# Heads enter attention in fours instead of pairs

## The reference, cut to what matters

```python
# block 1, 16 heads of 64 (256 keys are one block, so this is plain causal softmax): "moba"
p = softmax(where(k_pos <= q_pos, (q @ k.T) * 64 ** -0.5, -inf));  o = p @ v;  mix = o @ w_o

# block 2, heads 0 to 7, stick-breaking: "sb"
z = (q @ k.T) * 64 ** -0.5
log_keep = where(mask, log_sigmoid(-z), 0)                   # mask: key strictly before query
later = cumsum(log_keep, reverse=True) - log_keep            # sum over the later keys
w = where(mask, exp(log_sigmoid(z) + later), 0);  o = w @ v

# block 2, heads 8 to 15, forgetting attention: "fox" (q and k are normed per head)
z = (q @ k.T) * 64 ** -0.5 + F[query] - F[key]               # F: cumulative log of the forget gate
p = softmax(where(mask, z, -inf));  o = p @ v
mix = concat(all heads) @ w_o
```

## Time and profile before

| | |
|---|---|
| median of 3 runs | 814.82 us (813.75 to 815.11) |
| the profiled execution | 814.42 us, of which the span of the trace is 812.2 |
| busy in the span | TensorE 798.2, VectorE 647.5, ScalarE 483.8, GpSimd 21.1 us |
| granted TensorE clock | 0.997 of full speed on average |
| memory traffic | 179.44 MB, 221 GB/s on average |

### The profile page before, as it was taken

How to read it: one execution, slowest core, us unless ns; L and a number is a source line. 1 busy time by engine, 2 the same in 40 slices (tenths; PEclk the granted TensorE clock), 3 DMA queues, 4 the chain that set the end, 5 groups by cost and what they waited for, 6 DMA issues and landing times.

```text
span 812.2 us, 16860 instructions
## 1 busy us (share of the span) xinstructions
PE 798.2 (98%) x6810; PEld 777.2 (96%) x6810; DVE 647.5 (80%) x1385; ACT 483.8 (60%) x1008; POOL 21.1 (3%) x53
## 2 busy tenths in 40 slices
PE   8999999999999999999999999899999999999998
PEld 7999998999999999999999999889889999999998
DVE  5889887988899886999988887977667896775551
ACT  6755566776666566745554646665655775555440
POOL 1000000000000000000000000700000000000000
PEclk9999999999999999999999999999999999999999
DMA  9777683666656987499998887545334578655540
GB/s 292 261 240 241 219 286 113 206 203 208 206 191 199 324 299 261 157 322 325 360 327 297 298 259 223 163 135 175 124 109 152 167 261 271 209 184 196 194 157 27
DMA packets 150014, 179.44 MB, mean 221 GB/s; under 512 B 5681, under 2 KB 139569, under 8 KB 149937
## 3 DMA queue, kind: packets, MB, share of 16 engines
q1 hardware_dynamic: 147680, 177.22, 65.5%
q10 hardware_dynamic: 1232, 1.11, 0.4%
q0 software_dynamic: 1024, 0.03, 0.1%
HBM read 177.27 MB, written 1.05 MB: 220 GB/s over the span
## 4 chain that ended last, share of the span: by engine, by line
PE 77%; DVE 4%; ACT 3%; issue 1%; DVEq 0%; ACTq 0%
PE bank L1396 24%; PE bank L1399 23%; PE bank L1400 23%; DVE wlo L979 1%; PE bank L1385 1%; PE bank L1503 1%; PE bank L1387 1%; PE bank L1386 1%; PE bank L1487 1%; PE bank L1520 0%; PE bank L1417 0%; PE bank L1449 0%; ACT whi L736 0%; PE bank L1466 0%; DVE yb L1019 0%
## 5 line engine op out<-in xcount | busy, mean ns | idle before, releaser
L979 DVE TENSOR_TENSOR wlo<-raw,whi 128x512 fp32r<-128x512 f32 x528 | 342.9, 684 | 66.9 <-ACT whi L736 66.4
L736 ACT ACTIVATE whi<-raw 128x512 fp32r<-128x512 f32 x528 | 306.9, 622 | 96.6 <-PE bank L1400 85.4
L1396 PE MATMUL bank<-A,whi 128*128 128x256 f32 x1152 | 323.6, 281 | 2.8 <-DVE wlo L979 2.0
L1399 PE MATMUL bank<-A,whi 128*128 128x256 f32 x1152 | 319.5, 277 | 0.1
L1400 PE MATMUL bank<-A,wlo 128*128 128x256 f32 x1152 | 319.1, 277 | 0.0
L1396 PEld LDWEIGHTS bank<-A,whi 128*128 128x128 f32 x1152 | 217.3, 189 | 4.4 <-DVE wlo L979 2.2
L1399 PEld LDWEIGHTS bank<-A,whi 128*128 128x128 f32 x1152 | 217.2, 189 | 0.8 <-issue 0.5
L1400 PEld LDWEIGHTS bank<-A,wlo 128*128 128x128 f32 x1152 | 217.0, 188 | 0.0
L1396 PE MATMUL bank<-Hhi,whi 128*128 128x256 f32 x528 | 146.0, 276 | 0.0
L1400 PE MATMUL bank<-Hhi,wlo 128*128 128x256 f32 x528 | 145.7, 276 | 0.0
L1399 PE MATMUL bank<-Hlo,whi 128*128 128x256 f32 x528 | 145.7, 276 | 0.0
(11 more groups left out here) (160 smaller groups left out, 956.7 us busy)
## 6 DMA issues: line engine op xcount, KB each, us to landing
mring<-in_w_mod SPq DMA_DIRECT2D x72, 512.0 KB, 6.4
raw<-in_ffn_w_up SPq DMA_DIRECT2D x22, 1024.0 KB, 5.1
raw<-in_w_gate SPq DMA_DIRECT2D x22, 1024.0 KB, 5.6
raw<-in_w_up SPq DMA_DIRECT2D x22, 1024.0 KB, 5.8
raw<-in_w_down SPq DMA_DIRECT2D x16, 1024.0 KB, 5.8
raw<-in_w_in SPq DMA_DIRECT2D x12, 1024.0 KB, 5.8
raw<-in_moba_w_qkv SPq DMA_DIRECT2D x11, 1024.0 KB, 6.4
raw<-in_ffn_w_down SPq DMA_DIRECT2D x8, 1024.0 KB, 7.1
```

What stands on the lines that cost most here:

```text
L736: act.activation(whi[:, i % SPL, k0:k1, 0:width], raw[:, i % RAW, k0:k1, 0:width], ACT.Copy).then_inc(s_whi, 1)
L979: dve.tensor_tensor(lo, raw[:, i % RAW, k0:k1, 0:width], hi.bitcast(F32), ALU.subtract).then_inc(s_wlo, 1)
L1396: pe.matmul(o, hi, xh, start=kg == 0 and not (j and halved(g)), stop=False)
L1399: pe.matmul(o, hi, xl, start=False, stop=False)
```

## The change

Four heads enter together. `scores` multiplies all four in one step, first the one pair of heads, then the other; `values` does so too, into the two halves of `O_BANK`, with one copy by ScalarE and one by VectorE behind it. Only the fours that begin with head 12 have two `values` steps of two heads. The steps in between remain steps of one head, at ages given by the table `AGES`: for moba and fox as before (the second pair three turns after the first), for sb one head every second turn, with `values` at age 12. The next four enters when the one before has age 6 or more. `scores` waits until the banks of all four heads are free, and in qkv3 until the last group that used two banks is evicted (`last_raw`). FA and FB are cleared to zero and get ones in 4 rows at 0 and at 64, and their product takes 64 rows. `UNLOCK` and the due turn of `vturn` are moved by one or two turns. The core of the diff:

```diff
--- before.py
+++ after.py
@@
-LAST_AGE = 6
+AGES = {"sb": ((0, 2, 4, 6), (2, 4, 6, 8), (4, 6, 8, 10), 12), "moba": ((0, 0, 3, 3), (2, 3, 5, 6), (3, 4, 6, 7), 9)}
+AGES["fox"] = AGES["moba"]
-UNLOCK = {("qkv3", 512): 5, ("qkv3", 2048): 3, ("qkv3", 2304): 3}
+UNLOCK = {("qkv3", 512): 7, ("qkv3", 2048): 5, ("qkv3", 2304): 3}
@@ Plan.lay
         def advance(n, age):
             kind, ph, h = self.heads[n]
+            passes, sums, turned, last = AGES[kind]
+            early = h == 12
             if age == 0:
                 st.put("scores", n)
-            if age in (3, 4):
-                m = n + age - 3
-                st.put("later" if kind == "sb" else "turn", m)
-                self.w_of[m] = len(self.w_of) + 1
-            if age in (2, 3):
-                st.put("stsum" if kind == "sb" else "scale", n + age - 2)
-            if age == LAST_AGE:
-                while h // 2 not in v_ready:
-                    pend(force=True)
-                st.put("values", n)
-                o_ready.add(h // 2)
+            for first, size, at in ((n, 2, turned[1] + 2), (n + 2, 2, last)) if early else ((n, 4, last),):
+                if age == at:
+                    while h // 2 not in v_ready:
+                        pend(force=True)
+                    st.put("values", first, size)
+                    for k in range(first, first + size):
+                        self.values_of[k] = (first, size)
+                        o_ready.add(self.heads[k][2] // 2)
+            for k in range(4):
+                if age == turned[k]:
+                    st.put("later" if kind == "sb" else "turn", n + k)
+                    self.w_of[n + k] = len(self.w_of) + 1
+                if age == sums[k]:
+                    st.put("stsum" if kind == "sb" else "scale", n + k)
+            for k in range(4):
+                if age == passes[k]:
+                    st.put("passes", n + k)
@@ enter, attend
-            self.heads += [waiting.pop(0), waiting.pop(0)]
+            self.heads += [waiting.pop(0) for _ in range(4)]
...
-            if waiting and (not flight or flight[-1][1] > 2):
+            if waiting and (not flight or flight[-1][1] >= 6):
                 enter()
             turns[0] += 1
-            pend(not any(pair[1] in (3, 4) for pair in flight))
+            pend(not any(four[1] in AGES[self.heads[four[0]][0]][2] for four in flight))
...
-                    pending.append(("vturn", ph, base, turns[0] + 2))
+                    pending.append(("vturn", ph, base, turns[0] + 3))
@@ gpsimd, spread_f
-                pool.memset(FA[:, :, :].bitcast(F32), 1.0).then_inc(s_fset, 1)
-                pool.memset(FB[:, :, :].bitcast(F32), 1.0).then_inc(s_fset, 1)
+                pool.memset(FA[:, :, :].bitcast(F32), 0.0).then_inc(s_fset, 1)
+                pool.memset(FB[:, :, :].bitcast(F32), 0.0).then_inc(s_fset, 1)
                 pool.wait_ge(s_fset, 2)
+                for r0 in (0, 64):
+                    pool.memset(FA[r0:r0 + 4, :, :].bitcast(F32), 1.0).then_inc(s_fset, 1)
+                    pool.memset(FB[r0:r0 + 4, :, :].bitcast(F32), 1.0).then_inc(s_fset, 1)
+                pool.wait_ge(s_fset, 6)
@@ scalar, values (the vector engine's in the same way)
-            def values(n):
-                f = heads[n][2] // 2
-                need.wait_ge(s_val, n // 2 + 1)
-                act.activation(Ohi[:, f, :], banks[O_BANK][:, 0:S], ACT.Copy).then_inc(s_ohi, 1)
+            def values(n, size):
+                need.wait_ge(s_val, val_of[n])
+                o, src = heads_out(n, size)
+                act.activation(Ohi[:, o, :], src, ACT.Copy).then_inc(s_ohi, 1)
@@ tensor, scores
-                for m in (n - 4, n - 3):
+                for m in range(n - 4, n):
                     if m in soft:
                         need.wait_ge(s_exp, soft[m])
                     elif m in stick:
                         need.wait_ge(s_lb, stick[m])
+                if ph == "qkv3":
+                    emptied(need, last_raw)
...
+                    for two in (four[0:2], four[2:4]):
+                        for o0, o1, k0, q0 in ((P, 3 * P, 0, 0), (0, P, P, P)):
+                            for b, q, k in two:
+                                pe.matmul(b[:, o0:o1], k[:, k0:k0 + P], q[:, q0:S], start=q0 == 0, stop=False)
+                    for b, q, k in four:
+                        pe.matmul(b[:, 0:S], identb[:, :], negs[:, :].unsqueeze(1).broadcast_to([P, 2, P]), start=False,
+                                  stop=True).then_inc(s_scores, 1)
                     return
...
                 if kind == "fox":
...
-                            r = slice(64 * e, 64 * e + 4)
-                            ins = pe.matmul(pair[e][0][:, o0:o1], FA[r, i, q0:q0 + P], FB[r, i, 0:o1 - o0], start=False, stop=o0 > 0)
+                                ins = pe.matmul(two[e][0][:, o0:o1], FA[rows[e], i, q0:q0 + P], FB[rows[e], i, 0:o1 - o0], start=False, stop=o0 > 0)
@@ tensor, values
                 for t, o0, w0, w1 in ((0, 0, P, 3 * P), (1, P, 0, P)):
-                    for e in range(2):
-                        o, w = banks[O_BANK][64 * e:64 * e + 64, o0:S], W8[:, 2 * ((n + e) % 4) + 1, w0:w1]
-                        ins = pe.matmul(o, Vn[:, t, (h + e) * 64:(h + e) * 64 + 64], w, start=t == 0, stop=t == 1)
+                    for e in range(size):
+                        c = e // 2 * S
+                        o, w = banks[O_BANK][64 * (e % 2):64 * (e % 2) + 64, c + o0:c + S], W8[:, 2 * ((n + e) % 4) + 1, w0:w1]
+                        ins = pe.matmul(o, Vn[:, t, (h + e) * 64:(h + e) * 64 + 64], w, start=t == 0 and e < 2, stop=t == 1 and e >= size - 2)
```

More of the change, by code:

```diff
@@ L525, in build_program @@
         t_use = {step: k for k, step in enumerate(s for s in st.list if s[0] in ("turn", "later", "vturn", "qkn"))}
+        val_of = {n: nth("values", *plan.values_of[n]) for n in range(len(heads))}
+        val_of_tile = {(heads[n][1], heads[n][2] // 2): val_of[n] for n in range(len(heads))}
         soft = {n: k + 1 for k, n in enumerate(m for m, h in enumerate(heads) if h[0] != "sb")}
@@ L961, in _ @@
             part_of = {"hi": weights, "ain": a_in, "gq": norm_columns, "sq": squares, "norm": norm, "latey": late_hi, "modul": shift_hi,
[L962 removed]
+                       "ccol": condition, "evict": evict, "fpart": forget, "passes": first_pass, "turn": turned, "later": later,
                        "values": values, "vturn": v_turned, "qkn": qk_norm}
@@ L1314, in later, with values @@
                 dve.tensor_tensor(lb, lb, banks[T_BANK][:, 0:3 * P], ALU.add).then_inc(s_lsum, 1)
[L1316 to L1319, removed]
+            def values(n, size):
+                need.wait_ge(s_ohi, val_of[n])
+                o, src = heads_out(n, size)
+                dve.tensor_tensor(Olo[:, o, :], src, Ohi[:, o, :].bitcast(F32), ALU.subtract).then_inc(s_olo, 1)
             def qk_norm(base):
@@ L1332, in _ @@
                        "hcol": gates, "gq": first_columns, "mod": mod_dot, "modout": mod_out, "xscale": scale_x, "evict": evict, "fpart": forget,
-                       "scores": peaks, "scale": scale, "stsum": stick_sum, "later": later, "values": values, "qkn": qk_norm}
+                       "passes": peak, "scale": scale, "stsum": stick_sum, "later": later, "values": values, "qkn": qk_norm}
             for step in st.list:
@@ L1437, in scores @@
                     need.wait_ge(s_fmove, 16 * 32)
-                pair = [(head_bank(n + e), QKV[64 * e:64 * e + 64, place(ph, f), :], QKV[64 * e:64 * e + 64, place(ph, 8 + f), :]) for e in range(2)]
+                rows = (slice(0, 64), slice(64, P))
+                four = [(head_bank(n + e), QKV[rows[e % 2], place(ph, f + e // 2), :], QKV[rows[e % 2], place(ph, 8 + f + e // 2), :]) for e in range(4)]
                 if kind == "sb":
[L1440 to L1443, removed]
-                        ins = pe.matmul(b[:, 0:S], identb[:, :], negs[:, :].unsqueeze(1).broadcast_to([P, 2, P]), start=False, stop=True)
-                        ins.then_inc(s_scores, 1)
-                    return
@@ new lines, in scores @@
+                    for b, q, k in four:
+                        pe.matmul(b[:, 0:S], identb[:, :], negs[:, :].unsqueeze(1).broadcast_to([P, 2, P]), start=False,
+                                  stop=True).then_inc(s_scores, 1)
+                    return
+                for two in (four[0:2], four[2:4]):
+                    for o0, o1, q0 in ((0, S, P), (S, 3 * P, 0)):
+                        for b, q, k in two:
+                            ins = pe.matmul(b[:, o0:o1], q[:, q0:q0 + P], k[:, 0:o1 - o0], start=o0 == 0, stop=o0 > 0 and kind == "moba")
+                            if o0 > 0 and kind == "moba":
+                                ins.then_inc(s_scores, 1)
@@ L1488, in later, with values @@
                 pe.matmul(b[:, S:3 * P], negf[:, :], spl[:, 0:P], start=False, stop=True).then_inc(s_tpe, 1)
-            def values(n):
```

(3 more changed lines are left out.)

52 lines of the change are left out of this document (22 added, 30 removed).

## The result

The changed kernel takes 810.49 us (median of 5 runs, 810.36 to 811.46) where the kernel before takes 814.82: ratio 0.9954, 95% interval 0.9939 to 0.9968. That is 4.3 us less than the median of before, 3.7 by the ratio; forecast were 809.0 from a sum of 5.4 us less, with a range that holds the result. The trace of its profiled execution spans 808.7 us against 812.2. The blocks on PE came out as computed; what eats the gain is stops of PE, two kinds of which I had not seen coming.

What follows compares the result with a forecast made beforehand. TensorE (PE) was taken as the bound, its projection matmuls following without gaps. 5.2 of stream plus 1.5 and 1.5 of stops gone, less 2.0 and 0.8 of new waits, gave 5.4 us: 814.42 to 809.0, range 805.0 to 812.4.

Steps and rivals of the forecast that it cites:

- PE's stream, 5.2 us less: PE's attention blocks: moba scores 1.5 us less, values 1.7, stick-breaking scores 0.5, fox scores 1.5; 5.2 in all.
- Rival 2: In PE's blocks of four, each second pair pays its weight loads again; gain falls by 2.1 us, 811.1; chance 0.14.
- Rival 4: On PE, the shape is switched at each operand's change anyhow; only stick-breaking's stops go, 812.9 us; chance 0.04.
- Stops that go, 3.0: PE's two stops for stick-breaking's sum on VectorE go, 1.5 us; moba's stops at each four's first transposition go, 1.5 us.
- Stick-breaking's spreading: Stick-breaking passes one head every second turn, so PE's two stops for VectorE's sum go: 1.5 us less.
- New stops in moba, 2.0: PE waits 0.6 to 0.7 us per four for VectorE at the third and fourth transposition, last four excepted: 2.0 us.
- rival 1: In attention, VectorE catches up, so PE gets no new waits and fox loses its 0.7 too: 805.5 us; chance 0.2.
- rival 3: In fours, VectorE's pace holds PE, so the values block comes on top: slower, 816.4 us; chance 0.05.
- New stops in fox, 0.8, beside 0.7 that stay: In fox fours, PE's new waits for VectorE cost 0.8 us; the old first-transposition stops, 0.7, are not booked as gone.
- the prediction's 2.2 less 1.37: First fox four: stick-breaking values' copy, Olo and then the scale take about 2.2 us against a turn of 1.37.
- the V-turn: The stick-breaking heads' V-turn, where PE waits 1.60 us for VectorE: expected to stay within 0.2.

Runs made afterwards that it cites:

- its undoing: Changed kernel with scores in two blocks again, the second pair's block ahead of its first passes: 811.72 us, ratio 0.9969 to the kernel before.
- the relieved run of the changed kernel: Changed kernel with the first 12 modulation sums on VectorE computed over only 64 of 1024 columns (values wrong): 810.71 us, ratio 0.9957 to the kernel before.
- the other bank: Changed kernel with the q/k norm's products in the values' bank instead of the one shared with transpositions and cumulative sums: 809.26 us, ratio 0.9942 to the kernel before.
- the run with fours alone: Changed kernel with the old ages for stick-breaking fours, scores and values still in fours: 813.67 us, ratio 0.9999 to the kernel before.

## Why the prediction was right, and where it was not

*PE's stream, 5.2 us less: right.* Scores 1.71 for 1.75, values 1.65 for 1.66, stick-breaking 2.05 for 2.11, fox 2.13 for 2.10; with the prediction's own prices for pairs that makes 5.6. That a switch costs 0.4 us and a second pair little more than its streaming is shown by the block of four and by its undoing. Rival 2 (weight loads) falls: the second pair of scores costs 1.71 - 1.06 = 0.65, streaming alone is 0.64. Rival 4 falls with it.

By the rule of the Trainium skill (TensorE: Matmul & The Clock Gate, Part 3, The mechanism), that weights load beside running matmuls only where the row group differs, one would have looked for more here; in this kernel it shows nowhere, at 0.65 us for 0.64 of streaming. The Trainium skill's rule that a change of mode drains TensorE (TensorEngine Tiling, Key Properties) agrees with the trace once more at the third shape (0.19 us a block).

*Stops that go, 3.0: right.* The two at stick-breaking's sum and the first stops of the second to fourth moba four went; 0.25 of the first's is left. Stick-breaking's spreading was undervalued, though: against the same fours with the old ages it is worth 3.7 us (3.0 in the qkv3 stretch), not 1.5, since in fours the old ages make five stops.

*New stops in moba, 2.0: about right in size, wrong in cause.* They are there, so rival 1 falls, and are 2.8 by starts: 1.0 in the first four, 0.7 in the second and third, 0.1 in the last, and the first one's 0.25. The period was forecast at 21.98 and is 22.02 (the terms that the prediction lists add up to 21.91; the 0.07 more stands in none of its rows); the fourth scale ends 12.8 us after the scores' start (forecast 12.94), short of the 13.16 from which rival 3 would have made the kernel slower. But I put the stops down to VectorE's load, and the relieved run of the changed kernel contradicts that. The step that failed is the reading of a busy share: 7.95 of 8.50 did not say what happens if work leaves.

*New stops in fox, 0.8, beside 0.7 that stay: mis-sized.* By starts they are 2.5 in all: 0.7 at the first transposition after the stick-breaking values, close to what was computed (it went when these values moved a turn), 0.2 and 0.2, and the 1.36 at the third. The 0.8 is the prediction's 2.2 less 1.37, all of it at the first transposition; for the third, "the same stretch with less other DVE work", the sum has no term. Before that scale VectorE is busy from 552 on without a pause, after having waited in its queue for the values.

*Norms: not in the sum at all.* The prediction does not name them. With one cumulative sum in every second turn a norm can stand right ahead of one, in the same bank, with ScalarE busy in between; two of the four do. 1.9 us, of which the other bank gave back 1.0.

*The total: nearer than the account.* The result falls 1.5 us short of the forecast, but the sum of 5.4 was all for the attention stretches, and these gave 3.0: 2.4 short. The other microsecond, the sooner start and the half outside the span, was in nobody's sum; that part of the agreement is luck. The three misses, 1.0 in fox, 1.9 at the norms and 0.8 in moba, are 3.7. Against them stand 0.4 of stream and 0.2 at stick-breaking's sum beyond the forecast, and 0.3 at the V-turn (bracket 1.6 before, 1.3 after). The 0.4 that is left over is no more than what one trace can tell of a stretch.

## What to carry to other kernels

Where one engine is the bound and the others go through one common order, price a shorter stream by its blocks (that can be exact to hundredths of a microsecond) and then ask at each step that PE now reaches sooner which queue it depends on, and what stands ahead of that in the queue, rather than how busy the engine is. Grouping gave 1.3 us in moba, where nothing was in its way, and nothing in qkv3, where it met new stops; look at it by stretch, since the total of the run with fours alone (no change) hid a gain and a loss. The work that was left in two parts on purpose (values in front of a transposition) was worth more than its switch, because it filled a stop. A step in a shared buffer is finished when the slowest queue has read it: put it where nobody wants the buffer next, or give it its own.

## What the runs showed of the hardware

A second pair in the same shape costs its streaming only, 0.65 us for 0.64, although it loads weights for the same row halves again. A change from 64 rows to 4 rows with the same data costs 0.19 us per block, a bit under half of what a block of its own has beside its streaming (0.42). And 12 operations on VectorE, busy 94% of the stretch in question, cut from 1.22 to 0.22 us each, moved neither kernel's time out of its interval (ratios 0.9957 for 0.9954, and 1.0005). One 28 us window of unbroken projection matmuls, at a granted clock of 1.00, held 249 of them in one run and 241 in another: the same code runs at 0.113 or 0.117 us a matmul (by starts), and no run here shows what decides it.
